# A two-layer attention and mixer kernel: v projections by seven products, and the modulation products dealt evenly to the two layers

## What is computed

```python
# in each hybrid layer, h and w_in in float32, twelve chunks of 512 columns and a small one
h = rms_norm(x, g_pre)
p = h @ w_in
qa, ka, va, ga, qs, ks, vs, gs, qf, kf, vf, gf, ff = jnp.split(p, split_at, axis=-1)
# in the second part, once a layer, for the latent and the context stream
mod_l = jnp.split(jax.nn.silu(c) @ ada_w[layer] + ada_b[layer], 6, axis=-1)
mod_c = jnp.split(jax.nn.silu(c_ctx) @ ada_w[layer] + ada_b[layer], 6, axis=-1)
```

## Time and profile before

| | us |
|---|---|
| median of 3 runs | 3259.21 (3256.31 to 3259.44) |
| the profiled execution | 3255.98 |
| its span, first to last instruction | 3253.9 |
| projection stage of layer 0 | about 15 to 341 |
| projection stage of layer 1 | about 582 to 882 |

### The profile page before, as it was taken

How to read it: one execution, slowest core, us unless ns; L and a number is a source line. 1 busy time by engine, 2 the same in 40 slices (tenths; PEclk the granted TensorE clock), 3 DMA queues, 4 the chain that set the end, 5 groups by cost and what they waited for, 6 DMA issues and landing times.

```text
span 3253.9 us, 35548 instructions
## 1 busy us (share of the span) xinstructions
PE 3070.5 (94%) x14271; PEld 1622.1 (50%) x14271; DVE 1484.0 (46%) x2792; ACT 723.3 (22%) x1509; POOL 254.8 (8%) x171
## 2 busy tenths in 40 slices
PE   8899889999989899999998999999999888899998
PEld 5667544587644344456856533333335544444443
DVE  6894751876283334684575222222243762111112
ACT  1120550221153210212124110000014652111111
POOL 2433000434100000000001000000000000000000
PEclk9999999999999899999999999999999999999999
DMA  6453002455200321210422799888851003999997
GB/s 233 150 199 117 27 1 77 166 208 193 78 1 14 131 81 59 81 52 8 163 73 80 310 379 361 337 331 343 340 201 52 27 1 123 379 421 421 421 421 295
DMA packets 87621, 598.18 MB, mean 184 GB/s; under 512 B 10456, under 2 KB 11259, under 8 KB 16932
## 3 DMA queue, kind: packets, MB, share of 16 engines
q1 hardware_dynamic: 79776, 575.70, 44.5%
q10 hardware_dynamic: 5524, 12.35, 1.1%
q0 software_dynamic: 2160, 7.87, 0.6%
HBM read 590.64 MB, written 5.24 MB: 183 GB/s over the span
## 4 chain that ended last, share of the span: by engine, by line
PE 63%; DVE 7%; ACT 2%; issue 1%; DMA 0%; another core or an unknown queue 0%; DVEq 0%; SPq 0%; ACTq 0%; PEldq 0%
PE ps L1300 8%; PE ps L2669 7%; PE ps L2631 7%; PE ps L2648 3%; PE ps L2712 3%; PE ps L2682 3%; PE ps L2543 3%; PE ps L1033 3%; PE ps L2955 2%; PE ps L2526 2%; PE ps L2721 2%; PE ps L2442 2%; PE ps L1398 2%; PE ps L1638 2%; PE ps L3116 1%; PE ps L1450 1%
## 5 line engine op out<-in xcount | busy, mean ns | idle before, releaser
L583 PE MATMUL ps<-mem 128*128 128x256 f32 x1792 | 394.2, 382 | 12.5 <-DVE mem L607 12.4
L583 PEld LDWEIGHTS ps<-mem 128*128 128x128 f32 x1792 | 341.9, 191 | 66.7 <-DVE mem L607 15.7
L542 POOL TENSOR_TENSOR mem<-mem 128x512 f32<-128x512 f32 (+1 forms) x136 | 226.7, 1667 | 638.6 <-DVE mem L794 285.6
L2810 DVE TENSOR_TENSOR mem<-ps,mem 128x512 f32<-128x512 f32 x32 | 22.1, 692 | 547.3 <-PE ps L2631 313.7
L1300 PE MATMUL ps<-mem 128*128 128x512 f32 (+1 forms) x768 | 253.6, 492 | 2.9 <-ACT mem L1141 2.9
L700 DVE SCALAR_TENSOR_TENSOR mem<-mem 128x1024 f32<-128x1024 f32 x160 | 237.3, 1526 | 0.7 <-ACT mem L726 0.6
L2669 PE MATMUL ps<-mem 128*64 128x512 f32 x1024 | 223.3, 594 | 0.0
L2631 PE MATMUL ps<-mem 128*64 128x512 f32 x1024 | 222.5, 592 | 0.7 <-ACT mem L2568 0.7
L1300 PEld LDWEIGHTS ps<-mem 128*128 128x128 f32 x768 | 147.2, 193 | 108.6 <-issue 97.2
L1033 PE MATMUL ps<-mem 128*128 128x512 f32 x384 | 169.6, 597 | 1.8 <-DVEq L156 1.8
L661 PE MATMUL ps<-mem 128*128 128x512 f32 x384 | 165.8, 592 | 0.0
(11 more groups left out here) (413 smaller groups left out, 4074.6 us busy)
## 6 DMA issues: line engine op xcount, KB each, us to landing
mem<-in_moe_w SPq DMA_DIRECT2D x384, 1024.0 KB, 14.4
mem<-in_w_in SPq DMA_DIRECT2D x48, 1024.0 KB, 7.2
mem<-in_ada_w SPq DMA_DIRECT2D x48, 1024.0 KB, 4.9
mem<-in_hy_w_in SPq DMA_DIRECT2D x24, 1024.0 KB, 6.9
mem<-in_w_out SPq DMA_DIRECT2D x12, 1024.0 KB, 5.9
mem<-in_k_win_l SPq DMA_DIRECT2D x8, 1024.0 KB, 6.9
mem<-in_hy_w_out SPq DMA_DIRECT2D x8, 1024.0 KB, 4.9
mem<-in_sw_w_in SPq DMA_DIRECT2D x6, 1024.0 KB, 7.9
```

The source lines that it names most:

```text
L542: gp(out, x, y, op).then_inc(A.mark(sem), 1)
L583: m = mm(seven(l, j, i), x[:, k, :], y[:, k, :], start=(k == 0), stop=(k == 3))
```

## The change

The v chunks are made by seven products too. A v chunk is one block, not two pairs: each of the seven products has two units (u = 0 and 1, 128 tokens each), whose weights are a 128-token slice of the data's sum and whose moving operand is a 256-column sum of the chunk's weights (`WIDE_LEFT`, three places that overlay the six of `LEFT`). So a v block has 14 units of four matmuls with 256 moving columns, four 1024-wide sums on GpSimd, two copies on ACT and 16 additions on DVE (two for each of products 1 and 2 at its first tile, four for product 3 at the second, two at the third, four at the last). GpSimd's waits are now computed from the last product that used each place. The buffer `SUM` is gone; its partial sum lies in the destination.

The modulation products are dealt by slots: hybrid layer 0 works off slots 0 to 19, layer 1 slots 20 to 47, which is 80 products each. Within a layer a block's tile is spread evenly from 2 to 34. SP deals the slots to chunks by the same counts (2 or 3 a chunk in layer 0, 3 or 4 in layer 1). The biases of both layers are added once, at tile 35 of layer 1.

```diff
+        MOD_FIRST = 20
-        SUM = v(SUM_, 256)
+        WIDE_LEFT = [v(at, 4, 256) for at in (HT_ + 4096, HT_ + 5120, LEFT_)]
+        SEVEN_V = [4 * c for c in (2, 6, 10)]
+        BLOCKS = sorted(SEVEN + SEVEN_V)
+        products_of = lambda j: [(j, i, u) for i in range(7) for u in range(2 if j in SEVEN_V else 1)]
+        def wide_quarter(s, i, j):
+            return Wc[s][:, 4 * j:4 * j + 4, 256 * i:256 * i + 256]
...
+            free = [0] * 6
+            for j in BLOCKS:
...
+                if j in SEVEN_V:
+                    x, places = [WIDE_LEFT[i] for i in (1, 2, 0, 2)], ((2, 3), (4, 5), (0, 1), (4, 5))
+                SUMS = ((w(1, 0), w(1, 1), ALU.add, 2), (x[0], w(0, 0), ALU.subtract, 1),
+                        (w(0, 0), w(1, 0), ALU.subtract, 3), (w(0, 1), x[1], ALU.subtract, 5))
...
+                    if j in SEVEN_V:
+                        m = mm(seven(l, unit), y[:, k, u * P:(u + 1) * P], x[:, k, :], start=(k == 0), stop=(k == 3))
+                    else:
+                        m = mm(seven(l, unit), x[:, k, :], y[:, k, :], start=(k == 0), stop=(k == 3))
...
+                if i == 1:
+                    A.e.wait_ge(S["copied"], COPIED_NO[j, 0, u])
+                    add(C[1][0], unit, C[0][0])
+                if i == 3:
+                    add(C[1][1], unit, C[0][1], None)
+                    add(C[1][0], unit, C[1][0])
...
-                for b, z in MOD_OPS[l]:
-                    if j == 2 + 2 * b // 3:
-                        dve_mod_product(A, l, b, z)
+                for layer, b, z in MOD_OPS:
+                    at = layer * MOD_SLOTS + b // 2 - l * MOD_FIRST
+                    if 0 <= at < MOD_SPLIT[l] and j == 2 + (2 * at + b % 2) * 33 // (2 * MOD_SPLIT[l]):
+                        dve_mod_product(A, l, layer, b, z)
...
-                        for at in range(3 * c - 3, 3 * c):
-                            modulate(at)
+                        for slot in range(first + (last - first) * (c - 1) // 8, first + (last - first) * c // 8):
+                            modulate(slot)
```

More of the change, by code:

```diff
@@ L554, in pool_hyb_proj @@
                 s = PLACE[n]
[L555 to L563, removed]
@@ new lines, in pool_hyb_proj @@
+                SUMS = ((w(1, 0), w(1, 1), ALU.add, 2), (x[0], w(0, 0), ALU.subtract, 1),
+                        (w(0, 0), w(1, 0), ALU.subtract, 3), (w(0, 1), x[1], ALU.subtract, 5))
+                for i, (one, two, op, product) in enumerate(SUMS):
+                    until = max(free[place] for place in places[i])
+                    if until:
+                        A.e.wait_ge(S["product"], until)
+                    made(x[i], one, two, op, "filter_folded")
+                    for place in places[i]:
+                        free[place] = PRODUCT_NO[j, product, 1 if j in SEVEN_V else 0]
@@ L585, in pe_seven, with corners @@
                         m.then_inc(S["w_used"], 2)
                 m.then_inc(A.mark("product"), 1)
-        def act_seven(A, l, j):
[L590 to L593, removed]
+        def corners(j, u):
+            if j in SEVEN_V:
+                tiles = hyb_dest(j + u), hyb_dest(j + 2 + u)
+                return [[tile[:, 256 * i:256 * i + 256] for tile in tiles] for i in range(2)]
+            return [[hyb_dest(j + i)[:, 256 * k:256 * k + 256] for k in range(2)] for i in range(2)]
@@ L594, in act_seven @@
+        def act_seven(A, l, j):
+            for unit in products_of(j):
+                if unit[1] == 0:
+                    A.e.wait_ge(S["product"], PRODUCT_NO[unit])
+                    act(corners(j, unit[2])[0][0], seven(l, unit), ACT.Copy).then_inc(A.mark("copied"), 1)
+            if HK[j][1] in "gq":
                 fn, scale = {"g": (ACT.Silu, 1.0), "q": (ACT.Copy, 0.125)}[HK[j][1]]
@@ L599, in dve_seven, with add @@
         def dve_seven(A, l, j):
[L601 to L620, removed]
+            def add(out, unit, x, sem="product_read"):
+                A.e.wait_ge(S["product"], PRODUCT_NO[unit])
+                tt(out, seven(l, unit), x, ALU.add).then_inc(A.mark(sem), 1)
+            for unit in products_of(j):
+                _, i, u = unit
+                C = corners(j, u)
+                if i == 1:
+                    A.e.wait_ge(S["copied"], COPIED_NO[j, 0, u])
+                    add(C[1][0], unit, C[0][0])
+                if i == 2:
+                    if u == 0:
+                        A.e.wait_ge(S["product_read"], READ_NO[j, 1, 1 if j in SEVEN_V else 0])
+                    add(C[0][1], unit, C[1][0])
+                if i == 3:
+                    if u == 0:
+                        A.e.wait_ge(S["product_read"], READ_NO[j, 2, 1 if j in SEVEN_V else 0])
+                    add(C[1][1], unit, C[0][1], None)
+                    add(C[1][0], unit, C[1][0])
+                if i == 4:
+                    add(C[0][0], unit, C[0][0])
+                if i == 5:
+                    add(C[0][1], unit, C[0][1])
+                if i == 6:
+                    if u == 0:
+                        A.e.wait_ge(S["product_read"], READ_NO[j, 5, 1 if j in SEVEN_V else 0])
+                    add(C[1][0], unit, C[1][0])
+                if j in SEVEN_V:
+                    if u == 1 and i in (2, 3, 4):
+                        yield
+                elif i == 3:
+                    yield
         def hyb_dest(j):
@@ L703, in dve_mod_product, with dve_mod_bias @@
                 products[l] = A.last
[L705 to L710, removed]
+        def dve_mod_bias(A):
+            A.e.wait_ge(S["mod_used"], DEPTH * MOD_SLOTS)
+            for layer in range(DEPTH):
+                at = LS_ + layer * N_LV + LAYER_COLS["ada_b"][0]
+                for z, n in ((0, 48), (1, 48 if layer == 0 else 16)):
+                    x = v(MOD_ + layer * 96, 48, 2)[:, 0:n, z]
+                    tt(x, x, M[:, at:at + n], ALU.add).then_inc(A.mark(), 1)
         SQ = v(QT_, KD, 512)
```

110 lines of the change are left out of this document (59 added, 51 removed).

## The result

| | before | after |
|---|---|---|
| median of 20 runs, us | 3257.64 (3254.73 to 3262.88) | 3265.0 (3258.13 to 3270.92) |
| ratio of the two, 95% interval | | 1.0022 (1.0016 to 1.0029) |
| the profiled execution, us | 3255.98 | 3258.13 |
| its span, us | 3253.9 | 3256.3 |

The change makes the kernel 7.4 us slower. The profiled execution is the fastest of the changed kernel's runs, 6.9 us under their median, so the first profile shows too small a loss. A second profile of the changed kernel is in the first experiment.

A forecast was written before the change was run, and what follows sets the result against it. PE was taken to bound both projection stages, except where DVE falls seven products behind. Terms of -19.1 (PE), -2.8 (layer 0) and +19.6 (layer 1) gave -2.3 us, a median of 3257 us, range 3241 to 3270.

The forecast's parts named there:

- PE, six v chunks: Both projection stages: each v chunk falls from 27.46 to 24.27 us on PE, saving 19.1 us over six.
- loss in layer 0, less that of before: Layer 0's projection stage: PE loses 14.5 us behind DVE instead of 17.3, a gain of 2.8 us.
- loss in layer 1, less that of before: Layer 1's projection stage: PE loses 19.6 us behind DVE, where the trace before has 0.
- rival of bare weight loads: Six v blocks: weight loads don't overlap matmuls, 48 more each at 190 ns; +36 us, 3295 us; chance 0.01.
- v blocks run no faster on PE: V blocks: PE gains nothing there for some reason other than bare loads; +17 us, 3276 us; chance 0.02.
- price of GpSimd: Pairs of chunks 3 to 5: GpSimd's sums cost DVE 1.1 us in a usual pair.
- where DVE stands: Layer 1: DVE enters chunk 3 with 8.1 us lost; its next pairs take 18.7, 16.4, 14.2 and 13.0 us.
- SP's queue: Layer 1's chunks 3 and 9: weights queued behind modulation loads that wait for DVE; costed at nothing, cover 5 us.
- sign of being wrong: Layer 1: PE waiting there for GpSimd or for weights would show the forecast wrong; no size given.
- 3.7 us in chunk 6: Layer 0, chunk 6: 21.4 us of DVE's own work and about 6 of sums cost 3.7 us more.
- more meetings: Both stages: every wide sum stops DVE in full, pairs of chunks 3 and 4 pay 2.9; +16, 3275 us; chance 0.20.
- fewer meetings: Both stages: small sums cost nearly nothing, half the wide ones fall into waits and reads; -17, 3242 us; chance 0.37.

The follow-up runs named there:

- the first experiment: The changed kernel run again with no edit, for a second profile: 3268.65 us, ratio 1.0028 against the kernel before.
- the two kernels with short products: The changed kernel and the kernel before, each with modulation products over 64 of 1024 elements, the rest left out: 3221.47 and 3241.46 us.
- first regrouped run: The changed kernel with only SP's order regrouped, so no chunk's weights stand behind a modulation slot whose wait is late: 3267.59 us, ratio 1.0034.
- the sums were narrow: The changed kernel with GpSimd's sums of weights over 4 x 16 elements (layer 0 from chunk 2 on), all waits kept: 3232.89 us, ratio 0.9928.

## Why the prediction was wrong

It said 3257, no change, and the range 3241 to 3270 holds the time, but the kernel became slower by 7.4 us where the sum had it 2.3 us faster. To that side I had given only 0.23. The terms of the sum, in us, beside the lengths of the two profiles:

| term | forecast | first profile | second profile |
|---|---|---|---|
| PE, six v chunks | -19.1 | -19.8 | -19.8 |
| loss in layer 0, less that of before | 14.5 - 17.3 = -2.8 | 18.1 - 17.6 = +0.5 | 21.7 - 17.6 = +4.1 |
| loss in layer 1, less that of before | 19.6 | 23.7 - 0.4 = +23.3 | 26.0 - 0.4 = +25.6 |
| sum | -2.3 | +4.0 | +9.9 |

So two terms failed, each by 3 to 7 us.

- **What PE saves: right.** 20.0 us between the two kernels with short products, and 24.17 us in every v chunk without stalls. The rival of bare weight loads is refuted: 112 matmuls in 24.17 us. That v blocks run no faster on PE is refuted too.
- **Layer 0: the price of GpSimd, 1.1 us a pair, was too low.** It came from three steps of the kernel before. I left out the first pair of chunk 3, the one in which the sums of several pairs come together. By the excess of each product and rope instruction it cost DVE 4.6 us there, and 4.2 us in layer 1. In the changed kernel the pairs of chunks 3 to 5 in layer 0 cost DVE 13.0 us, where my steps held some 11. A third pair shows it: it took 19.9 us (134.36 to 154.29) and not 16.5, since four sums ran together when its weights had landed:

```profile
135.19 7.88 POOL L555 TENSOR_TENSOR mem<-mem 128x512 f32<-128x512 f32 x4 [6.98 <-DMA mem<-in_w_in]
```

(GpSimd's timeline of the changed kernel, layer 0.) And DVE entered chunk 3 10.5 us behind PE (105.06 against 94.58), where I had 8.5. Chunks 3 to 5 then took 90.6 us and not 82 to 84.

- **Layer 1: where DVE stands was right, its end was not.** DVE's four pairs came within 1.4 us of the times forecast, so the moved products as a cost were right. Some of that closeness is luck: the steps between the pairs were 20.1, 15.4 and 14.2 us against 18.7, 16.4 and 14.2, and the errors cancel. But I had the loss end with chunk 4 (chunk 5 was to catch up, chunk 6 to fit). PE lost 2.5 us in chunk 5 in a wait for GpSimd, and 3.1 us (first profile) and 4.1 (second) in chunks 6 to 9.
- **SP's queue: wrong as a term.** I costed it at nothing, and named PE's waiting for GpSimd in layer 1 as a sign of being wrong. That sign came: PE waited 5.1 us for GpSimd's sums there (4.1 in pairs, 1.0 in a v block), with weights landing late, and DVE 10.3 us for modulation loads. The term does not add up with the others, though: with weights in time (first regrouped run) the kernel is no faster, since the sums then meet DVE elsewhere.
- **Chunks 6 to 9 of layer 0.** I had 3.7 us in chunk 6. The first profile has nothing there, the second 5.3 us in chunks 6 to 9.
- **The rivals.** The one that came true is "more meetings", at half its size. Its opposite, "fewer meetings", rested on layer 1's 0.8 us a pair, which leaves out the same first pair. I had an argument against it and gave it 0.37 nevertheless.
- **The scale.** The forecast came from one execution. The losses vary from one to the next: the changed kernel's two profiles differ by 6 us in the two stages, as much as either failed term.

What stays open: which of the meetings could be avoided by the order alone. A run that lays GpSimd's sums in time beside DVE's reads of PSUM was not tried. Nor was another order on DVE: in each of the four pairs of chunks 3 and 4 DVE stands idle for 3.82 us until ACT has swapped the strips of the rope (15.3 us a layer in the changed kernel's waits), while its modulation products stand behind the rope. What it would give to put them into that wait, no run shows.

## What to carry to other kernels

Before an engine's work is split into more and smaller pieces, ask how late the engine that frees its buffers is, and what hides that: seven banks with a plain tile of 6.9 us each let it be up to 48 us late (an estimate, 7 x 6.9), seven with a product of 1.74 us only 12, and v blocks alone took layer 0's loss from 17.6 to 36.4 us. Put such a change first where the freeing engine has nothing else to do (here chunk 10: 6 us for one line), and lay the side work by the room of each stretch and not by an even count; the count to lay is that of products and that of transfers, both. A price of interference is to be read where the engine is late, with the worst pair in it. It can't be read from the busy shares of the page.

## What the runs showed of the hardware

DVE and GpSimd hold each other up. A product takes 1.22 us alone, 2.28 beside a 512-wide sum (itself 1.27 alone) and 3.35 beside a 1024-wide one (2.35), so it grows by nearly the length of the sum. The mean of the group fell from 1618 to 1290 ns once the sums were narrow. The Trainium skill, "SBUF — State Buffer", section "Who interferes with whom", says so for a DVE instruction with two inputs in SBUF and a GpSimd instruction that reads SBUF, and that one with at most one SBUF input, outside the modes that use both ports, does not contend. The trace agrees: four additions with one input in PSUM take 1.66 us beside sums (at 105.06 in the changed kernel) and without them (at 121.24). What I had not expected is the size at the level of the kernel: up to 32 us of its time (3265.0 to 3232.9, and more against the second median) hang on GpSimd's sums, though GpSimd is busy for 10% of the span and DVE for 47%.
